# Turning one head's normalised output through DRAM and VectorE's 32x32 transposes instead of TensorE, with the scores and the query products one chunk earlier

## The reference, cut to what matters

```python
out = (jnp.einsum('bhlm,bhmv->bhlv', scores, v)
       + jnp.einsum('bhld,bhdv->bhlv', q, S) * q_decay[:, :, None])
...
yn = ((yf - mu) * lax.rsqrt(var + GN_EPS)).astype(h.dtype)
yn = yn.transpose(0, 2, 1, 3).reshape(B, L, RET_V)
return (jax.nn.silu(g) * yn) @ w_out, S_new
```

## Time and profile before

| | |
|---|---|
| median of 3 runs | 1660.34 us (1660.22 to 1661.06) |
| the profiled execution | 1660.56 us |
| its span, first to last instruction | 1659.0 us |
| TensorE busy | 1639.8 us (99%), 10857 products |
| VectorE busy | 1050.4 us (63%) |
| ScalarE busy | 595.6 us (36%) |
| mean granted TensorE clock | 0.997 |

### The profile page before, as it was taken

One profiled execution on the slowest core, in us unless ns is written; L12 is line 12 of the kernel. 1 busy time (PEld: TensorE's weight loads), 2 busy tenths in 40 slices (PEclk: granted clock), 3 DMA queues, 4 the chain that ended last, 5 costly groups with the idle time before them and its releaser, 6 DMA issues.

```text
span 1659.0 us, 30163 instructions
## 1 busy us (share of the span) xinstructions
PE 1639.8 (99%) x10857; PEld 1579.8 (95%) x10857; DVE 1050.4 (63%) x1677; ACT 595.6 (36%) x820; POOL 163.0 (10%) x240
## 2 busy tenths in 40 slices
PE   8999999999999999999999999999999999999996
PEld 8999989989999999999998998999999999999996
DVE  6566556556656656656655655977766666666465
ACT  4333333333333333333233333543333334343334
POOL 1001101101100100100100110510000000000243
PEclk9999999999999999999999999999999999999998
DMA  9647847846855864884794793445744444444443
GB/s 323 217 142 260 322 139 260 310 141 221 318 196 171 310 230 154 283 293 142 262 324 136 256 325 113 148 143 179 254 153 151 151 140 146 146 150 145 145 146 112
DMA packets 127223, 338.45 MB, mean 204 GB/s; under 512 B 27344, under 2 KB 45904, under 8 KB 127136
## 3 DMA queue, kind: packets, MB, share of 16 engines
q1 hardware_dynamic: 106928, 263.63, 47.9%
q0 software_dynamic: 20208, 73.55, 12.3%
HBM read 280.08 MB, written 46.28 MB: 197 GB/s over the span
## 4 chain that ended last, share of the span: by engine, by line
PE 97%; ACT 1%; DVE 1%; POOL 1%; issue 0%; DMA 0%; SPq 0%; POOLq 0%; ACTq 0%; DVEq 0%
PE proj L1341 25%; PE proj L1342 25%; PE proj L1346 25%; PE proj L1479 5%; PE proj L1487 4%; PE proj L1480 4%; PE qs L1438 2%; PE side L1325 1%; PE side L1370 1%; PE side L1327 1%; PE side L1326 1%; PE proj L1508 1%; POOL residual L500 1%; PE side L1332 0%; PE qs L1443 0%
## 5 line engine op out<-in xcount | busy, mean ns | idle before, releaser
L1341 PE MATMUL proj<-x_hi,w_hi 128*128 128x322 f32 (+2 forms) x2496 | 757.9, 314 | 0.2 <-DVE qk_raw_or_gate L916 0.2
L1342 PE MATMUL proj<-x_lo,w_hi 128*128 128x322 f32 (+2 forms) x2496 | 754.0, 312 | 0.0
L591 ACT CAST w_hi<-w_raw 128x1024 fp32r<-128x1024 f32 x412 | 431.9, 1049 | 582.9 <-PE proj L1342 383.6
L840 DVE TENSOR_TENSOR w_lo<-w_raw,w_hi 128x1024 fp32r<-128x1024 f32 x412 | 507.6, 1235 | 142.5 <-ACT w_hi L591 88.6
L1341 PEld LDWEIGHTS proj<-x_hi,w_hi 128*128 128x128 f32 x2496 | 470.8, 189 | 5.5 <-issue 4.4
L1342 PEld LDWEIGHTS proj<-x_lo,w_hi 128*128 128x128 f32 x2496 | 470.1, 188 | 0.4
L1346 PE MATMUL proj<-x_hi,w_lo 128*128 128x322 f32 (+2 forms) x2496 | 425.5, 313 | 0.0
L1346 PEld LDWEIGHTS proj<-x_hi,w_lo 128*128 128x128 f32 x2496 | 386.6, 189 | 0.0
L1479 PE MATMUL proj<-qk_or_z,w_hi 128*128 128x322 f32 x480 | 147.1, 317 | 2.3 <-DVE qk_or_z L1051 1.4
L1480 PE MATMUL proj<-qk_or_z,w_hi 128*128 128x322 f32 x480 | 144.0, 310 | 0.0
L873 DVE SCALAR_TENSOR_TENSOR state_update<-state_update,state_decay_of_head,side 128x512 f32<-128x512 f32 x128 | 94.1, 735 | 17.3 <-PE side L1370 14.5
(11 more groups left out here) (222 smaller groups left out, 1303.1 us busy)
## 6 DMA issues: line engine op xcount, KB each, us to landing
w_raw<-w_head SPq DMA_DIRECT2D x252, 512.0 KB, 4.4
w_raw<-w_conv SPq DMA_DIRECT2D x128, 512.0 KB, 3.5
state_update<-s_in POOLq DMA_DIRECT2D x64, 512.0 KB, 7.4
s_out<-state_update POOLq DMA_DIRECT2D x64, 512.0 KB, 6.1
te_for_q_or_prompt_state<-s_in SPq DMA_DIRECT2D x32, 512.0 KB, 8.2
w_raw<-w_cout SPq DMA_DIRECT2D x32, 512.0 KB, 3.6
v_scratch<-v_turned_or_y_norm SPq DMA_DIRECT2D x32, 176.0 KB, 5.4
v_rows<-v_scratch SPq DMA_DIRECT2D x8, 512.0 KB, 4.8
```

The source lines that it names most:

```text
L591: act.copy(w_hi[:, i % SPL, :], w_raw[:, i % RAW, :]).then_inc(w_h.sem, 1)
L840: TT(w_lo[:, i % SPL, :], w_raw[:, i % RAW, :], f(w_hi[:, i % SPL, :]), ALU.subtract).then_inc(w_l.sem, 1)
L1341: mm(bank[:, 0:n], wh[:, k, :], rhs_h(k), start=(first and k == 0), stop=False)
L1342: x = mm(bank[:, 0:n], wh[:, k, :], rhs_l(k), start=False, stop=False)
```

## The change

The normalised rows `y_n` go out to a DRAM tensor in three transfers and come back in four as `y_b`, in which 32 tokens by 32 features blocks lie so that VectorE's 32x32 transpose gives features by tokens. VectorE turns each block j with one instruction into PSUM, and TensorE's transposes go. The turned features come in another order than before, so the host lays out the gate's and the output projection's weights in that order. The scores move from behind chunk 17 to behind 16, the big stop from 18 to 17, the normalisation forward with them. The two halves of the prompt state both stand behind 23. ScalarE rounds chunk 24 and VectorE makes its `w_lo` ahead of z instead of behind it. The rows for the state products go out one or two places earlier in SP's list.

```diff
-QS_CHUNK = 18
+QS_CHUNK = 17
-EARLY = (4, 16, 17)
+EARLY = (4, 16, 17, 23)
-VS_AT = {22: (8, 9, 10, 11), 23: (0, 1, 2), 24: (3, 4, 5), 25: (6, 7)}
+VS_AT = {21: (8, 9, 10, 11), 22: (0, 1, 2, 3, 4, 5, 6, 7)}
+Y_OUT = Y_BACK = 24
...
+        y_b = vt_yn[:, :].rearrange("p (t n) -> p t n", t=YB)
+        y_dram = nc.dram_tensor("y_scratch", [YB, 32, DV], F32).ap()
+        yt_bank = [bank_r[2], bank_r[0], bank_r[1], bank_q]
...
+                    if i == Y_OUT:
+                        for n, t in enumerate((0, 2, 1)):
+                            sp.wait_ge(y_nm.sem, y_nm.at(h, n + 1))
+                            sp.dma_start(y_dram[4 * t:4 * t + 4, :, :].rearrange("a p n -> (a p) n"),
+                                         y_n[:, t, :]).then_inc(yd_out.sem, 16)
+                    if i == Y_BACK:
+                        sp.wait_ge(yd_out.sem, yd_out.at(h, yd_out.per))
+                        for a in range(4):
+                            sp.dma_start(y_b[32 * a:32 * a + 32, :, :],
+                                         y_dram[:, :, P * a:P * a + P].rearrange("t p e -> p t e")).then_inc(yd_in.sem, 16)
                     load_chunk(0, h, CPH, i, w_head[h, i])
...
                     if i == 24:
-                        z_round(3)
-                    if i in (23, 24) and not last:
-
-                        d = i - 23
+                        z_round(2, 3)
+                    for d in range(DKB) if i == 24 and not last else ():
                         act.wait_ge(st_done.sem, st_done.at(h, d + 1))
                         act.copy(pst[:, d, :], st_bank[d][:, :]).then_inc(st_read.sem, 1)
                     if i == 23:
-                        z_round(0, 1, 2)
+                        z_round(0, 1)
...
+                    def turned(j):
+
+                        dve.transpose(yt_bank[j][:, 0:3 * P].rearrange("p (t e) -> p t e", e=32),
+                                      y_b[:, :, 32 * j:32 * j + 32]).then_inc(yt_done.sem, 1)
...
+                    if i == 23:
+                        dve.wait_ge(yd_in.sem, yd_in.at(h, yd_in.per))
+                        turned(0)
+                        turned(1)
+                        gated(0)
+                        turned(2)
+                        gated(1)
+                        z_rest(0)
+                        turned(3)
+                        gated(2)
+                        z_rest(1)
+                        z_rest(2)
+                    if i == 24:
+                        gated(3)
+                        z_rest(3)
...
-                    if i == 17:
+                    if i == 16:
                         pe.wait_ge(q_l.sem, q_l.at(h))
...
-                    if i == 23:
-                        y_turn(3)
-                    if i in (22, 23) and not last:
-
-                        d = i - 22
+                    for d in range(DKB) if i == 23 and not last else ():
```

More of the change, by code:

```diff
@@ L1012, in side @@
                             TT(a_lo[0:rows, at], tmp[0:rows, m % 2, 0:n], f(a_hi[0:rows, at]), ALU.subtract).then_inc(a_l.sem, 1)
-                    if i == 19:
+                    if i == 18:
                         dve.wait_ge(s_new.sem, s_new.at(h, 0))
                         dve.tensor_copy(sd_h[:, :], sdec[:, bass.ds(h, 1)]).then_inc(sd_set.sem, 1)
[L1017 to L1020, removed]
+                    if i == 18:
+                        for n, t in enumerate((0, 2, 1)):
+                            dve.wait_ge(y_done.sem, y_done.at(h, n + 1))
                             if t == 2:
@@ L1030, in side @@
-                    if i == 20:
+                            dve.bn_aggr(mv[:, t, :], stat[:, t, :]).then_inc(y_ag.sem, 1)
                         dve.wait_ge(y_ag.sem, y_ag.at(h, 3))
                         dve.tensor_scalar(gvar[:, :], mv[:, :, 1], GN_EPS, None, add).then_inc(y_ve.sem, 1)
-                    if i == 21:
+                    if i == 19:
                         dve.wait_ge(y_rs.sem, y_rs.at(h))
[L1035 to L1051, removed]
+                        for t in (0, 2, 1):
+                            dve.tensor_scalar(y_n[:, t, :], y_bank[t][:, :], mv[:, t, 0:1], rstd[:, t:t + 1],
+                                              ALU.subtract, ALU.mult).then_inc(y_nm.sem, 1)
@@ new lines, in turned, with gated @@
+                    def turned(j):
+                        dve.transpose(yt_bank[j][:, 0:3 * P].rearrange("p (t e) -> p t e", e=32),
+                                      y_b[:, :, 32 * j:32 * j + 32]).then_inc(yt_done.sem, 1)
+                    def gated(j):
+                        dve.wait_ge(yt_done.sem, yt_done.at(h, j + 1))
+                        dve.wait_ge(p_act.sem, p_act.at(h, 1 + j))
+                        if j >= 2:
+                            dve.wait_ge(z_l.sem, z_l.at(h, j - 1))
+                        c0, c1 = CUT, CUT + Y_TAIL
+                        TT(tmp[:, j % 2, 0:Y_TAIL], yt_bank[j][:, c0:c1], gate[:, j, 0:Y_TAIL], ALU.mult)
+                        groups = yt_bank[j][:, c1:c1 + 96].rearrange("p (c i) -> p c i", i=32)[:, :, META:]
+                        rest = lambda ap: ap.rearrange("p (c i) -> p c i", i=META)
+                        TT(rest(tmp[:, j % 2, Y_TAIL:N]), groups, rest(gate[:, j, Y_TAIL:N]), ALU.mult).then_inc(z_f.sem, 1)
@@ new lines, in z_rest @@
+                    def z_rest(j):
+                        dve.wait_ge(z_h.sem, z_h.at(h, j + 1))
+                        TT(z_lo[:, j, :], tmp[:, j % 2, 0:N], f(z_hi[:, j, :]), ALU.subtract).then_inc(z_l.sem, 1)
+                    if i == 23:
[10 more added lines that the diff above has]
+                        z_rest(2)
@@ L1055, in head @@
                 for i in range(CPH):
-                    if i == 24:
-                        side(i)
+                    if i and i != 24 and not (first and i < 4):
                         rest_chunk(0, h, CPH, i)
[L1061 to L1064, removed]
+                    if i == 23:
+                        rest_chunk(0, h, CPH, 24)
+                    side(i)
                     for back, t in due(KU_AT, i, first, last):
@@ L1378, in head @@
             def head(h, first, last=False):
[L1379 to L1385, removed]
-                        for t in range(3):
-                            c0, rows = QRY[t][0], Y_ROWS[t]
-                            x = turn(bank_r[j % 3][:, c0:c0 + rows], y_n[0:rows, t, P * j:P * j + P])
-                        x.then_inc(yt_done.sem, 1)
                 def side(i):
@@ L1447, in side @@
                         pe.wait_ge(a_l.sem, a_l.at(h, 3))
[L1448 to L1452 removed]
+                        at, kr = A_AT[2], KEY[2][1]
+                        for t in (0, 2, 1):
+                            if t == 2:
+                                x = three(bank_q[:, :], a_hi[0:kr, at:at + SW], a_lo[0:kr, at:at + SW], v_hi[0:kr, 2, :],
+                                          v_lo[0:kr, 2, :], False, True)
+                            for m in range(t + 1) if t < 2 else ():
+                                own = A_AT[m] + P * t - CUT - SC[m][0]
+                                x = three(bank_r[t][:, :], a_hi[:, own:own + P], a_lo[:, own:own + P],
                                           v_hi[:, m, :], v_lo[:, m, :], m == 0, m == t)
                             x.then_inc(y_done.sem, 1)
[L1455 to L1458 removed]
                     for back, t in due(KV_AT, i, first, last):
                         kv_multiply(h, t, back, last and not back)
[L1461 to L1462 removed]
                 def out(i):
@@ L1764 @@
         parts.append(part.reshape(HEADS, n * 2, P, HALF))
-    wo = A(w_ret_out)[0].reshape(HEADS, DVB, P, KT // 2, 2 * P).transpose(0, 3, 2, 1, 4)
+    wo = A(w_ret_out)[0].reshape(HEADS, 4, DVB, 32, KT // 2, 2 * P).transpose(0, 4, 1, 3, 2, 5)
     parts.append(wo.reshape(HEADS, 8, P, HALF))
```

38 lines of the change are left out of this document (12 added, 26 removed).

## The result

The changed kernel takes 1667.13 us (median of 5 runs, 1666.02 to 1669.90), the kernel before 1660.34 us on the same chip: ratio 1.0043, 95% interval 1.0032 to 1.0054. It is slower by 0.43%, where 1652.7 us was forecast, and lies above the range (1649.9 to 1658.5). The profiled execution took 1667.13 us, with a span of 1665.6 us against 1659.0.

The account below looks back on a forecast made before the run. TensorE, holding 97% of the chain that ended last, was taken as the bound. Seven heads at 1.11 us less the last head's 0.16 gave 7.6 us, so 1652.7 us was forecast, range 1649.9 to 1658.5.

Parts of the forecast that it names:

- TensorE's side: Between chunks 22 and 24: transposes go, leaving chunk 23 and two half states, so TensorE reaches chunk 24 after 6.79 us.
- The scores' wait: Behind chunk 16: the scores need `q_lo`, so TensorE loses 0.14 us a head.
- A transpose of 384 columns from SBUF to PSUM: VectorE's turning of y ahead of chunk 24: 0.58 us each, next instruction after 0.51.
- the forecast's main term: From chunk 22 to chunk 24's 16 products: 1.25 us gained in a middle head, 1.11 after the scores' loss.
- Rival 1: VectorE bounds chunk 24: at 0.84 us a turning instead of 0.51, z is 1.3 us later, 1663.3 us; 7%.
- The step that failed: Chunk 24's load behind y's DRAM trip: issued at E + 10.7, landed at E + 14.5, slack 2.4 us.
- rival 2: SP holds back chunk 24's load: 0.7 us late gives 1658, 2.2 us late 1670; decides near a 5.7 us landing; 12%.
- The last head: No state there before: products end at 9.53 us against 9.51; with the scores it loses 0.16 us.
- The sum: All eight heads: 7.8 us gained in seven, 0.16 lost in the last, together 7.6 us.

Follow-up runs that it names:

- e4: The kernel before with only the scores moved behind chunk 16, the big stop behind 17 and y's normalisation one place earlier; TensorE still turns y: 1662.97 us.
- e1: The changed kernel, but SyncE issues chunk 24's load between y's three stores and its wait for their landing, not behind the four returns: 1654.64 us.
- e7: The kernel of e1, with 14 unneeded products on TensorE between chunks 23 and 24 of the last head: 1652.69 us.
- e6: The changed kernel, but GpSimd loads the next head's table behind the prompt state's store, some 15 us later, not beside y's stores: 1657.34 us.
- e2: The changed kernel, but GpSimd instead of SyncE issues y's three stores and four returns, behind its pow for y's scales: 1681.40 us.
- e8: The changed kernel, but VectorE makes `w_lo` of chunk 19 ahead of y's last statistics, not behind them: 1663.37 us.
- e3: The changed kernel, but ScalarE and VectorE round chunk 24 after z, as the kernel before did; the load stays late: 1653.64 us.

## Why the prediction was wrong

**What it had right.** TensorE's side came out to the hundredth: 6.80 us from chunk 22 to chunk 24. The scores' wait was 0.17 us (e4) for 0.14. A transpose of 384 columns from SBUF to PSUM was put at 0.58 and measured 0.566:

```profile
L1053 DVE STREAM_TRANSPOSE side<-v_turned_or_y_norm x24: 548/566/587, 105.3 to 1033.7; 128x384 f32<-128x384 f32 x24
```

From the first transpose to the last z the changed kernel takes 6.25 us (633.10 to 639.35), the prediction 6.56 (1.33 to 7.89). With the load out of the way a middle head gains 1.19 us (e1, e7) for 1.11, so the forecast's main term holds. Rival 1 is out. The 0.566 us for three blocks of 128x128 is 0.19 each, float32 from SBUF into PSUM. The prediction's 0.20 for 128 columns is not a row of its own: it is 0.55 x 128 / 352 from the 352 columns of the earlier trace rows, which go from PSUM to SBUF.

**The step that failed** is "The load of chunk 24, which stands behind them in SP's list, is issued at E + 10.7 and lands 3.8 us later, at E + 14.5 ... Slack 2.4 us". E, the end of the stop, is 612.19 in the changed kernel's fifth head, the start of the next chunk. There the last y was ready at 618.80 (618.00 + 0.80), E + 6.6 and not 5.9 (GpSimd's root took 1.0 us longer). From there the stores had landed 4.7 us later and not 2.3. The returns and the next issue took 2.1 and not 2.5. The load went out at E + 13.4 and needed 5.2 us and not 3.8: E + 18.6. Of 4.1 us too late the landing of the stores is 2.4, the load 1.4, y 0.7, the returns -0.4. The slack of 2.4 is used up, and the other 1.7 us are what VectorE and TensorE wait: the head is 132.5 us long and 130.8 in e1.

```profile
612.19 0.31 PE L1370 MATMUL proj<-x_hi,w_hi 128*128 128x322 f32 x1
```

```profile
618.00 0.80 DVE L1048 TENSOR_SCALAR v_turned_or_y_norm<-side,gn_mean_var,gn_rstd 128x512 f32<-128x512 f32 x1
```

The slack itself was sized right, to E + 16.9. In the last head the load landed at E + 16.8, and the transposes began 19.2 us behind E, as in every head of e1; in the other seven it landed between E + 17.5 and E + 19.8. In these seven the transposes began 11.7 us later than in e1, added up, of the 13.4 us by which the heads are longer. Most of the rest is in the sixth head, where the clock fell.

This is rival 2, to which I had given 12%, by a shorter route than I had put it: it was to decide at a landing near 5.7 us, and decided at 4.7, because y and the load were late too.

Why the sizes were too small: 2.3 us came from the output's stores, at the end of the program, and 3.8 from two loads of the kernel before, beside rows of v of 64 KB each and a table that landed in 3.2 us. The trip brings more: the stores of y run beside chunk 23's load and the table (0.7 us of the median by e6), which itself now takes 5.1 us, and chunk 24's load comes right behind four returns, with four more loads behind it in 8 us. How far the load's 5.2 us come from these neighbours is not shown. In e1, between the stores and the returns, it took 5.1 in the fifth head and 3.7 in the last, which loads no table; in the changed kernel's last head, behind the returns, 5.1. v's way to DRAM, 5.4 us in the earlier trace rows, was the nearer row, and I had put it aside.

**The last head** was forecast at -0.16 us. Its chain of z came as forecast: the last block was ready 7.66 us after chunk 22 in e1 (1017.32 to 1024.98), 7.89 in the sum. But with the transposes gone TensorE is idle there for 2.2 us (0.65 + 0.71 + 0.86) where it was 1.8 before (0.55 + 1.21), its clock falls to 0.50, and the products behind the wait take 1.35 + 0.95 us longer. e7 gives that back. I had treated the wait as the only cost of waiting.

**The sum made good.** e7, which is the changed kernel with one transfer moved and the last head filled, takes 1652.69 us; the forecast for the change was 1652.7. That the two agree so closely is partly luck, since e7 is another kernel and its heads gain a little more than forecast. Its gain over the kernel before is 0.47% (0.35% to 0.60%).

**What stays open:** why single stores land in 2.9 and others in 5.0 us in one kernel, what makes the load take 5.2, why the returns are late in e2, which wait of TensorE costs it the clock, and e8's time.

## What to carry to other kernels

A load that is queued behind a wait on another transfer is as late as that transfer's slowest landing (y's stores had landed 4.7 us after the last y); put it ahead of the wait (12.5 us here, e1), or take the work that doesn't need it out from behind it (13.5 us, e3). Price a transfer by a row with the neighbours that it will have, and if the only such row is longer than the slack, the case is not settled. Another engine's transfer can be that neighbour: moving the table alone took back 9.8 us (e6). Where waits of TensorE get longer, count the products behind them at the clock that it may have then: at 0.50, e1's 18 took 5.00 us (2.85 + 2.15) where e7's took 2.76 (1.57 + 1.19).

## What the runs showed of the hardware

- GpSimd's root of 128x3 elements took 1.88 us where VectorE had begun `w_lo`, from two operands in SBUF, 0.08 us before it, and 0.88 us where VectorE made none beside it (e8). The program has no semaphore between the two. In the kernel before, where `w_lo` began 0.23 us behind the root, they took 1.23 and 0.88 us, as if alone.
- The same four returns landed in 6.3 us where GpSimd issued them and in 4.0 where SyncE did (medians, e2 and the changed kernel), and the kernel took 1681.4 us. That GpSimd's queue is the cause is not shown.
- TensorE, busy for 2.36 us of 4 in e1's last head, was granted 0.50 in the next 4 us, in which it was busy throughout; with 14 unneeded products in the gap it kept 1.00, and the stretch to the program's end was 2.5 us shorter (e7). In the kernel before it was busy for 2.25 us of 4 in the same place and kept 1.00.
